# Four of eight pairs of k tiles by seven block products in nine feed-forward groups, with GpSimd making most of the weight sums

## The chip, the cores and the metric

One core of one Trainium2 chip runs the whole kernel. The metric is the device time of one execution in microseconds (us). The engines are TensorE (PE in the profile, its weight loads PEld), VectorE (DVE), ScalarE (ACT), GpSimd (POOL) and SyncE (SP), which issues the weight transfers.

## The reference, cut to what matters

A decoder layer on 256 tokens of width 2048. After the mixer (head groups of mLSTM and retention, one input and one output projection), which the change leaves alone, comes the feed-forward part, of width 5632:

```python
h = rmsnorm(x, g_ffn_pre[l])
ff = (jax.nn.silu(h @ w_gate[l]) * (h @ w_up[l])) @ w_down[l]
x = x + rmsnorm(ff, g_ffn_post[l])
```

All tensors are float32. The change touches only how `h @ w_gate` and `h @ w_up` are computed.

## The kernel before

**Numbers in two parts.** Every float32 matrix product is made from three products of rounded parts. ScalarE rounds a weight tile into `w_hi`, VectorE subtracts (`w_lo = raw - w_hi`), and TensorE adds hi by hi, hi by lo and lo by hi in PSUM. A piece of 1024 weight columns per partition is called a sub; `w_hi` and `w_lo` hold four subs each (`AHEAD` = 4), so ScalarE may round sub m when TensorE has finished sub m-4 (`sub_done`), VectorE follows (`hi_done`), and TensorE follows VectorE (`lo_done`). Each engine works strictly in the order in which the program is written.

**Groups and units.** The feed-forward part has eleven groups of 512 columns of `w_gate` and `w_up`. Group 0 is plain. In groups 1 to 10 the sixteen k tiles (128 rows of the weights each) are taken as eight pairs, the units. A unit's weights are one chunk of `raw` (four chunks, 1 MB each, refilled by SyncE when `lo_done` says that a chunk was used): a quarter each of two `w_up` tiles (blocks b12, b22) and two `w_gate` tiles (b11, b21).

- An R unit is plain: 2 subs, each of 12 matmuls of 512 columns, 24 in all.
- An S unit uses the Strassen-Winograd scheme on the 2x2 blocks (two token tiles by two k tiles, two k tiles by gate and up): 7 block products of 3 matmuls, 21 in all, in 4 subs of 6, 3, 6 and 6 matmuls. The first two subs (b22 and b11, then b21) use the weights as they are. The last two need four sums of weight blocks, which `weight_sums` makes on VectorE, in place in `raw`, after the second sub. Sums of the token tiles are made once (`seven_sums`, `seven_lo`).

Before, `UNITS = "RRSRRSRR"`: two S units in a group, 20 subs. The products of sums gather in their own four PSUM banks over the S units of a group, and `partial_sums` (four VectorE adds of 128x512) folds them after the last S unit; TensorE may start the next group's first matmul only then (`part_done`), since that writes to those banks. The next group's first subs carry the finishing work of the group before: `up_sums`, `gate_sums`, the silu on ScalarE, `gated`, eight TensorE transposes after sub 1 (`turned_ff`), then `turned_hi` and `turned_lo`. The first product of a sum in the next group waits for `turned_lo` (`ff_lo`), which empties the banks of the transposes.

GpSimd does nothing in the feed-forward part but to issue one DMA. After the groups comes the product with `w_down`, plain.

The waits that bind VectorE to ScalarE in an S unit, in `unit_hi`:

```python
act.wait_ge(sub_done, ff_base(i) + (m - 3))
...
act.wait_ge(t_ready, 4 * i + (2 * SEVEN.index(n) + piece - 5))
```

Of the kernel before, what the change touches and what calls it, by code (L numbers as in the profile page):

```python
# [55 lines left out]
UNITS = "RRSRRSRR"  # L56
UNIT_SUBS = {"R": 2, "S": 4}
UNIT_BASE = [sum(UNIT_SUBS[kind] for kind in UNITS[:n]) for n in range(len(UNITS) + 1)]
FF_SUBS = UNIT_BASE[-1]
LAST_S = UNIT_BASE[UNITS.rindex("S") + 1]  # L60
SEVEN = [n for n, kind in enumerate(UNITS) if kind == "S"]
SUB_LIST = [(n, piece) for n, kind in enumerate(UNITS) for piece in range(UNIT_SUBS[kind])]
R_DOWN = R_FF + 2 + (FF_GROUPS - 1) * FF_SUBS // 8
RAW_DOWN = R_FF + 2 * FF_GROUPS
DOWN_SUBS = KF // 2
N_SUBS = 8 * R_DOWN + 4 * DOWN_SUBS
# [26 lines left out]
def ff_base(i):  # L93

    return FF_SUBS * i + (FF_FIRST - FF_SUBS)


def sum_banks(i_odd):

    return (4, 0) if i_odd else (0, 4)  # L100
# [62 lines left out]
def hybrid_layer(nc, x, positions, g_mix_pre, w_in, conv_w, conv_b, b_igate, b_fgate, g_mlstm_head,  # L163
                 g_ret_head, w_out, g_mix_post, g_ffn_pre, w_gate, w_up, w_down, g_ffn_post,
                 inv_freq, out):
    with ExitStack() as ctx:  # L166
# [59 lines left out]
        sb("early_tiles", [P, KF - 8, 2 * SEQ], stack=spare)  # L226
        s_whole = sb("s_whole", [P, 2, 2, SEQ], stack=spare)
        s_sum = sb("s_sum", [P, 2, 4, P], stack=spare)
# [12 lines left out]
        def ff(t):  # L241

            return part[:, 2 * t + 1, :]

# [151 lines left out]
        def _(sp):  # L396
            def load(rnd, q, src, wait=True, free=FREE):

                if wait:
                    sp.wait_ge(lo_done, 8 * (rnd - 1) + free[q])  # L400
# [67 lines left out]
            def second_half(i):  # L468
                for n in range(4, 8):
                    unit_rows(i, n, ff_base(i) + UNIT_BASE[n - 3])  # L470
# [3 lines left out]
            with sp.Fori(1, FF_GROUPS - 1) as i:  # L474
                second_half(i)
                for n in range(4):
                    unit_rows(i + 1, n, ff_base(i) + UNIT_BASE[n + 5])
            second_half(FF_GROUPS - 1)
            for n in range(4 * KF // 4):
                g, k = divmod(n, KF // 4)  # L480
                load(R_DOWN + n // 4, n % 4, rows(w_down, 4 * k, 4, 512 * g, 512))
# [9 lines left out]
        def _(pool):  # L491
# [34 lines left out]
            pool.wait_ge(sub_done, 8 * R_DOWN)  # L526
# [4 lines left out]
        def _(act):  # L531
# [314 lines left out]
            def unit_hi(i, m):  # L846

                n, piece = SUB_LIST[m]
                q, arrived = n % 4, 16 * (n // 4)
                act.wait_ge(sub_done, ff_base(i) + (m - 3))  # L850
                dst, cols = w_hi[:, m % AHEAD, :], slice(SUB * (piece % 2), SUB * (piece % 2 + 1))
                if piece == 0:
                    act.wait_ge(raw_up[q], 32 * i + (arrived - 16))
                if UNITS[n] == "R":
                    if piece == 1:
                        act.wait_ge(raw_full[q], 32 * i + (arrived + 16 * (R_FF + 1)))
                elif piece == 0:
                    act.wait_ge(raw_full[q], 32 * i + (arrived + 16 * (R_FF + 1)))
                    cols = slice(512, 512 + SUB)
                elif piece == 1:  # L860
                    dst, cols = w_hi[:, m % AHEAD, 0:512], slice(512 + SUB, 2 * SUB)
                else:
                    act.wait_ge(t_ready, 4 * i + (2 * SEVEN.index(n) + piece - 5))
                act.activation(dst, raw[:, q, cols], ACT.Copy).then_inc(hi_done, 1)  # L864

            def ff_group(i, odd, first=False):

                _, s0 = sum_banks(odd)
                for m in range(FF_SUBS):
                    unit_hi(i, m)  # L870
                    if m == 0 and first:
                        act.wait_ge(s_summed, 2)
                        for j in range(2):
                            act.activation(s_hi[:, j], s_sum[:, j], ACT.Copy).then_inc(s_rounded, 1)
# [4 lines left out]
                act.activation(part[:, 0, :], bank[:, s0 + 2, :], ACT.Copy).then_inc(p1_out, 1)  # L879
# [5 lines left out]
            ff_group(FF_GROUPS - 1, False)  # L885


            def down_hi(rnd, s):

                rnd, s = rnd + s // 8, s % 8  # L890
                act.wait_ge(raw_full[s // 2], 16 * (rnd + (RAW_DOWN - R_DOWN + 1)))
                act.activation(w_hi[:, s % AHEAD, :], raw_sub(rnd, s)[1], ACT.Copy).then_inc(hi_done, 1)  # L892

            def ahead(rnd, s):

                act.wait_ge(sub_done, 8 * rnd + s + 1)
                down_hi(rnd, s + AHEAD)

            for s in range(-AHEAD, 8):
                ahead(R_DOWN, s)  # L900
# [5 lines left out]
            for g in range(4):  # L906
                full, end = divmod(DOWN_SUBS * (g + 1) - 1, 8)
                with act.Fori(max(3 * g, 1), full) as r:
                    for s in range(8):
                        ahead(r + R_DOWN, s)  # L910
                for s in range(8 if g < 3 else 8 - AHEAD):
                    ahead(R_DOWN + full, s)
# [8 lines left out]
        def _(dve):  # L921
# [429 lines left out]
            def up_sums(i, c0):  # L1351

                dve.wait_ge(part_done, 2 * i)
                dve.wait_ge(sub_done, ff_base(i) + (FF_SUBS - 1))
# [3 lines left out]
            def gate_sums(i, c0):  # L1358

                dve.wait_ge(sub_done, ff_base(i) + FF_SUBS)  # L1360
# [34 lines left out]
            def seven_lo(j):  # L1395
# [20 lines left out]
            def unit_lo(i, m):  # L1416

                n, piece = SUB_LIST[m]
                part_, cols = slice(0, SUB), slice(SUB * (piece % 2), SUB * (piece % 2 + 1))
                if UNITS[n] == "S" and piece < 2:  # L1420
                    cols = slice(512, 512 + SUB) if piece == 0 else slice(512 + SUB, 2 * SUB)
                    part_ = slice(0, SUB) if piece == 0 else slice(0, 512)
                dve.wait_ge(hi_done, ff_base(i) + (m + 1))
                dve.tensor_tensor(w_lo[:, m % AHEAD, part_], raw[:, n % 4, cols],  # L1424
                                  w_hi[:, m % AHEAD, part_].bitcast(F32), ALU.subtract).then_inc(lo_done, 1)
                if UNITS[n] == "S" and piece == 1:
                    weight_sums(i, n)

            def partial_sums(i, s0):
# [3 lines left out]
                dve.wait_ge(sub_done, ff_base(i) + LAST_S)  # L1433
# [8 lines left out]
            def ff_group(i, odd, first=False):  # L1442

                c0, s0 = sum_banks(odd)
                for m in range(FF_SUBS):
                    if m == 2 and not first:
                        up_sums(i - 1, s0)
                    if m == 3 and not first:
                        gate_sums(i - 1, s0)
# [5 lines left out]
                    unit_lo(i, m)  # L1455
                    if m == 1 and first:
                        seven_lo(0)
                    if m == 2 and first:
                        seven_lo(1)
# [8 lines left out]
            for s in range(AHEAD):  # L1468
                lo(R_FF + 1, s + AHEAD)
                if s % 2:  # L1470
                    seven_sums(s // 2)
# [5 lines left out]
            ff_group(FF_GROUPS - 1, False)  # L1477


            for s in range(-AHEAD, 8):  # L1480
                if s == -2:
                    up_sums(FF_GROUPS - 1, 0)
                if s == -1:
                    gate_sums(FF_GROUPS - 1, 0)
                if s == 0:
                    gated(FF_GROUPS - 1)
                lo(R_DOWN, s + AHEAD)
                if s == 1:
# [20 lines left out]
        def _(pe):  # L1509
# [417 lines left out]
```

## Time and profile before

| | us |
|---|---|
| median of 3 runs (lowest, highest) | 1218.34 (1218.07, 1218.73) |
| the profiled execution | 1218.53 |
| its span, first to last instruction | 1216.8 |
| TensorE busy | 1205.2 (99%) |
| VectorE busy | 856.8 (70%) |
| ScalarE busy | 640.5 (53%) |
| GpSimd busy | 15.3 (1%) |

The profiled execution lies 0.2 us from the median, and 1.7 us of it are outside the span. A busy share is an average over all stages; what a stage is worth is read from the stretch of time in which it runs. The feed-forward groups 1 to 10 run from about 530 to 960 us.

### The profile page before, as it was taken

To read this page: it belongs to the slowest core of one execution; us is meant where nothing else is said; L and a number is where in the kernel's file an instruction comes from. 1 tells how busy PE (TensorE), PEld (TensorE's weight loads), DVE (VectorE), ACT (ScalarE), POOL (GpSimd) and SP (SyncE) were. 2 spreads that over 40 slices of the span, in tenths; PEclk is the share of its full clock that TensorE was granted. 3 is DMA by queue.
4 is the path that set the end of the run, shared out by engine and by line. 5 is a ranking of instruction groups with operands and counts; after the bars stand their busy time and mean duration, and the time that the engine had idled before them with its cause. 6 is when DMAs were issued, how large, how long until landed. Compare 5 with 4: busy or idle time off the path is not lost.

```text
span 1216.8 us, 16089 instructions
## 1 busy us (share of the span) xinstructions
PE 1205.2 (99%) x5839; PEld 1012.9 (83%) x5839; DVE 856.8 (70%) x1133; ACT 640.5 (53%) x841; POOL 15.3 (1%) x35
## 2 busy tenths in 40 slices
PE   8999999999999999999999999999999999999997
PEld 7888888888888888888888888888888888888886
DVE  6657877877777655768888888888878844444444
ACT  5654666475664645655455555545555544343432
POOL 2000200000000000000000000000000000000000
PEclk9999999999999999999999999999999999999999
DMA  8657868768686556455556456565645765555651
GB/s 314 211 148 158 206 152 167 171 137 218 160 197 193 198 183 208 161 185 205 175 173 241 142 211 230 176 205 175 211 168 187 262 206 178 205 189 191 203 177 69
DMA packets 121840, 229.59 MB, mean 189 GB/s; under 512 B 7360, under 2 KB 24000, under 8 KB 121280
## 3 DMA queue, kind: packets, MB, share of 16 engines
q1 hardware_dynamic: 121504, 226.85, 60.0%
q0 software_dynamic: 288, 2.10, 0.4%
q8 instruction: 30, 0.49, 0.2%
q14 instruction: 18, 0.15, 0.0%
HBM read 226.83 MB, written 2.10 MB: 188 GB/s over the span
## 4 chain that ended last, share of the span: by engine, by line
PE 98%; DVE 1%; DMA 1%; SPq 0%; ACT 0%; DVEq 0%; issue 0%
PE bank L1511 96%; PE bank L1809 1%; DMA resid<-in_x 1%; PE bank L1516 0%; PE bank L1725 0%; DVE w_lo L934 0%; DVE h L961 0%; DVE resid L1276 0%; PE bank L1782 0%; DVE hT L947 0%; DVE ff_out L1269 0%; ACT bank L749 0%; DVEq L166 0%; ACT hT L586 0%; DVE hT L968 0%
## 5 line engine op out<-in xcount | busy, mean ns | idle before, releaser
L934 DVE TENSOR_TENSOR w_lo<-raw,w_hi 128x1024 fp32r<-128x1024 f32 x260 | 317.2, 1224 | 249.5 <-ACT w_hi L544 128.6
L1511 PE MATMUL bank<-w_hi,h2T 128*128 128x512 f32 x1216 | 383.8, 390 | 0.0
L864 ACT ACTIVATE w_hi<-raw 128x1024 fp32r<-128x1024 f32 x200 | 201.6, 1018 | 197.9 <-PE bank L1511 167.8
L1424 DVE TENSOR_TENSOR w_lo<-raw,w_hi 128x1024 fp32r<-128x1024 f32 x200 | 229.3, 1169 | 65.4 <-ACT w_hi L864 62.7
L544 ACT ACTIVATE w_hi<-raw 128x1024 fp32r<-128x1024 f32 x172 | 181.0, 1059 | 173.9 <-PE bank L1511 156.7
L1511 PE MATMUL bank<-hT,w_hi 128*128 128x512 f32 x768 | 271.7, 397 | 0.0
L1511 PEld LDWEIGHTS bank<-w_hi,h2T 128*128 128x128 f32 x1216 | 228.3, 188 | 47.1
L1511 PE MATMUL bank<-w_lo,h2T 128*128 128x512 f32 x588 | 228.8, 389 | 0.0
L1511 PE MATMUL bank<-w_hi,ffT 128*128 128x512 f32 x704 | 217.3, 389 | 0.0
L1511 PE MATMUL bank<-hT,w_lo 128*128 128x256 f32 x768 | 214.6, 279 | 0.0
L1511 PEld LDWEIGHTS bank<-hT,w_hi 128*128 128x128 f32 x768 | 144.0, 187 | 32.4
L892 ACT ACTIVATE w_hi<-raw 128x1024 fp32r<-128x1024 f32 x88 | 93.4, 1061 | 138.7 <-PE bank L1511 138.6
L1511 PEld LDWEIGHTS bank<-w_hi,ffT 128*128 128x128 f32 x704 | 132.1, 188 | 27.6
L1511 PEld LDWEIGHTS bank<-hT,w_lo 128*128 128x128 f32 x768 | 145.0, 189 | 0.0
L1511 PE MATMUL bank<-w_lo,ffT 128*128 128x512 f32 x352 | 136.9, 389 | 0.0
L1511 PEld LDWEIGHTS bank<-w_lo,h2T 128*128 128x128 f32 x588 | 110.4, 188 | 22.6
L1511 PE MATMUL bank<-w_hi,hT 128*128 128x512 f32 x256 | 81.3, 393 | 0.8 <-DVE w_lo L934 0.8
L1511 PE MATMUL bank<-w_hi,mixT 128*128 128x512 f32 x256 | 80.1, 391 | 0.0
L1511 PEld LDWEIGHTS bank<-w_lo,ffT 128*128 128x128 f32 x352 | 66.1, 188 | 13.5
L1511 PEld LDWEIGHTS bank<-w_hi,hT 128*128 128x128 f32 x256 | 48.1, 188 | 11.4 <-issue 1.2
L1511 PEld LDWEIGHTS bank<-w_hi,mixT 128*128 128x128 f32 x256 | 48.1, 188 | 10.3 <-DVE mixT L1219 0.4
L1511 PE MATMUL bank<-w_lo,hT 128*128 128x512 f32 x128 | 49.8, 389 | 0.0
(203 smaller groups left out, 898.1 us busy)
## 6 DMA issues: line engine op xcount, KB each, us to landing
raw<-in_w_in SPq DMA_DIRECT2D x63, 1024.0 KB, 10.2
raw<-in_w_down SPq DMA_DIRECT2D x44, 1024.0 KB, 5.0
raw<-in_w_up SPq DMA_DIRECT2D x80, 512.0 KB, 4.0
raw<-in_w_gate SPq DMA_DIRECT2D x80, 512.0 KB, 4.9
raw<-in_w_out SPq DMA_DIRECT2D x16, 1024.0 KB, 5.0
raw<-in_w_gate SPq DMA_DIRECT2D x4, 1024.0 KB, 5.3
raw<-in_w_up SPq DMA_DIRECT2D x4, 1024.0 KB, 6.6
resid<-in_x SPq DMA_DIRECT2D x2, 1024.0 KB, 7.2
```

The lines of the kernel that those rows point to most:

```text
L544: act.activation(part_of(w_hi, rnd, s), src, ACT.Copy).then_inc(hi_done, 1)
L864: act.activation(dst, raw[:, q, cols], ACT.Copy).then_inc(hi_done, 1)
L892: act.activation(w_hi[:, s % AHEAD, :], raw_sub(rnd, s)[1], ACT.Copy).then_inc(hi_done, 1)
L934: dve.tensor_tensor(part_of(w_lo, rnd, s), raw_sub(rnd, s)[1], part_of(w_hi, rnd, s).bitcast(F32), ALU.subtract).then_inc(lo_done, 1)
L1424: dve.tensor_tensor(w_lo[:, m % AHEAD, part_], raw[:, n % 4, cols], w_hi[:, m % AHEAD, part_].bitcast(F32), ALU.subtract).then_inc(lo_done, 1)
L1511: return pe.matmul(out_, lhsT, rhs, start=start, stop=stop, skip_group_check=True)
L1809: ins = pe.transpose(bank[:, b0 + j // 2, c:c + P], ff(t)[:, j * P:(j + 1) * P], ident)
```

## The change

- `UNITS` becomes a `Plan` per group: `RSRSRSSR` in groups 1 to 9 (four S units, the last two in a row, 24 subs) and `RSRSRRRR` in group 10 (two S units, 20 subs).
- The sums are made in another order: b12 = b22 - b12 first, as soon as the chunk has landed and without a wait for the subs; b11 = b12 + b11 after the unit's first sub; b21 = b21 - b11 after the second; b22 = b22 - b11. Third and fourth sub take the blocks in another pairing.
- GpSimd makes all four sums in the S units 1, 3 and 5, and b12 and b22 in unit 6. VectorE makes b11 and b21 of unit 6. That is 14 sums of a group on GpSimd and 2 on VectorE, where 8 were on VectorE. The sums of group 10 are all GpSimd's.
- ScalarE's rounding of an S unit's third sub waits for b11 and b21, the fourth for b22 (in unit 6: b12 and b11, then b22 and b21).
- `partial_sums` of group i is no longer at the end of its group on VectorE but in group i+1, between the subs 0 and 1; ScalarE's copy of the first product moves likewise.
- The wait for `turned_lo` stands before the fourth sub of the first S unit, which is sub 5 of the group (before: before its first sub, sub 4).
- Token sums are made for four pairs instead of two, once.
- The loads wait for the chunk's use by the new counts.

The core of the diff:

```diff
-UNITS = "RRSRRSRR"
+SEVEN = (1, 3, 5, 6)
+SUMS_BY_POOL = (4, 4, 4, 2)
...
+FULL = Plan("RSRSRSSR")
+FINAL = Plan("RSRSRRRR")
...
+            def weight_sums(i, j):
+
+                n = SEVEN[j]
+                b12, b22, b11, b21 = (raw[:, n % 4, 512 * c:512 * (c + 1)] for c in range(4))
+                made = sums_made(i, j)
+                pool.wait_ge(raw_up[n % 4], 32 * i + 16 * (n // 4 - 1))
+                pool.tensor_tensor(b12, b22, b12, ALU.subtract).then_inc(t_ready, 1)
+                if j == 3:
+                    pool.wait_ge(t_vector, 2 * i - 1)
+                    pool.tensor_tensor(b22, b22, b11, ALU.subtract).then_inc(t_ready, 1)
+                    return
+                pool.wait_ge(lo_done, ff_base(i) + (FULL.base[n] + 1))
+                pool.wait_ge(t_ready, made + 1)
+                pool.tensor_tensor(b11, b12, b11, ALU.add).then_inc(t_ready, 1)
+                pool.wait_ge(lo_done, ff_base(i) + (FULL.base[n] + 2))
+                pool.wait_ge(t_ready, made + 2)
+                pool.tensor_tensor(b21, b21, b11, ALU.subtract).then_inc(t_ready, 1)
+                pool.tensor_tensor(b22, b22, b11, ALU.subtract).then_inc(t_ready, 1)
...
+                elif piece >= 2 and j == 3:
+                    act.wait_ge(t_ready, sums_made(i, j) + (piece - 1))
+                    act.wait_ge(t_vector, 2 * i + (piece - 3))
+                elif piece >= 2:
+                    act.wait_ge(t_ready, sums_made(i, j) + (piece + 1))
...
-                dve.wait_ge(lo_done, ff_base(i) + (UNIT_BASE[n] + 2))
-                dve.tensor_tensor(b11, b12, b11, ALU.subtract).then_inc(t_first, 1)
-                dve.wait_ge(t_first, 4 * i + (2 * j - 3))
-                dve.tensor_tensor(b12, b22, b12, ALU.subtract).then_inc(t_first, 1)
-                dve.wait_ge(t_first, 4 * i + (2 * j - 2))
-                dve.tensor_tensor(b22, b22, b11, ALU.subtract).then_inc(t_ready, 1)
-                dve.wait_ge(t_ready, 4 * i + (2 * j - 3))
-                dve.tensor_tensor(b21, b21, b22, ALU.subtract).then_inc(t_ready, 1)
...
-                for m in range(FF_SUBS):
+                for m in range(plan.subs):
+                    if m == 1 and not first:
+                        partial_sums(i - 1, FULL, c0)
                     if m == 2 and not first:
-                        up_sums(i - 1, s0)
+                        up_sums(i - 1, FULL, s0)
...
-                partial_sums(i, s0)
...
+                    pe.wait_ge(lo_done, ff_base(i) + (m + 1))
+                    if first and piece == 3:
+                        pe.wait_ge(ff_lo, 2 * i)
```

Where the weight sums stand. VectorE before, second S piece of the first S unit of a group in the loop and the sums behind it (`raw<-raw`):

```order
L1424 TENSOR_TENSOR w_lo<-raw,w_hi 128x512
L1408 TENSOR_TENSOR raw<-raw 128x512
L1409 ISA
L1410 TENSOR_TENSOR raw<-raw 128x512
L1411 REGISTER_ALU
L1412 TENSOR_TENSOR raw<-raw 128x512
L1414 TENSOR_TENSOR raw<-raw 128x512
```

GpSimd after, the first S unit of a group in its loop (before, there was nothing):

```order
L583 TENSOR_TENSOR raw<-raw 128x512
L588 ISA
L589 ISA
L590 TENSOR_TENSOR raw<-raw 128x512
L591 REGISTER_ALU
L592 REGISTER_ALU
L593 TENSOR_TENSOR raw<-raw 128x512
L594 TENSOR_TENSOR raw<-raw 128x512
```

The four sums have moved to GpSimd; on VectorE the third sub's subtraction now stands directly behind the second's.

The start of a group on VectorE, before (the first row that writes `part` is `up_sums`):

```order
L1424 TENSOR_TENSOR w_lo<-raw,w_hi 128x1024
L1423 REGISTER_ALU
L1424 TENSOR_TENSOR w_lo<-raw,w_hi 128x1024
L1353 ISA
L1354 ISA
L1356 TENSOR_TENSOR part<-part,bank 128x512 x2
L1423 REGISTER_ALU
L1424 TENSOR_TENSOR w_lo<-raw,w_hi 128x1024
```

and after:

```order
L1494 TENSOR_TENSOR w_lo<-raw,w_hi 128x1024
L1515 ISA
L1517 TENSOR_TENSOR part<-part,bank 128x512
L1518 ISA
L1519 TENSOR_TENSOR part<-part,bank 128x512
L1521 TENSOR_TENSOR part<-part,bank 128x512
L1522 TENSOR_TENSOR part<-part,bank 128x512
L1492 REGISTER_ALU
L1494 TENSOR_TENSOR w_lo<-raw,w_hi 128x1024
L1439 REGISTER_ALU
L1441 TENSOR_TENSOR part<-part,bank 128x512 x2
```

The four adds of `partial_sums` (L1517 to L1522) now stand between the first two subs of the next group, ahead of `up_sums` (L1441).

## Rows read from the trace of the kernel before

**Rows 1.** The page: busy time by engine, and the chain that ended last.

```profile
PE 1205.2 (99%) x5839; PEld 1012.9 (83%) x5839; DVE 856.8 (70%) x1133; ACT 640.5 (53%) x841; POOL 15.3 (1%) x35
...
PE 98%; DVE 1%; DMA 1%; SPq 0%; ACT 0%; DVEq 0%; issue 0%
```

**Rows 2.** Busy time of each engine in one whole group of the loop.

```profile
core 0: us, PE busy (x) PEld busy (x) DVE busy (x) ACT busy (x) POOL busy (x), PEclk, DMA share, GB/s
651.30:694.36 43.06, 43.06 (x196) 35.74 (x195) 35.83 (x41) 22.96 (x25) 0.00 (x0) 1.00 0.57 195
```

**Rows 3.** The same view for 60 us of the `w_down` stage, plain matmuls only.

```profile
1000.00:1060.00 60.00, 60.00 (x266) 49.67 (x266) 28.17 (x24) 24.68 (x27) 0.00 (x0) 1.00 0.58 193
```

**Rows 4.** VectorE's instructions by form in that group: line, shapes, count | busy, mean ns.

```profile
L1424 DVE TENSOR_TENSOR w_lo<-raw,w_hi 128x1024 fp32r<-128x1024 f32 x18 | 21.6, 1222 | 4.1 <-ACT w_hi L864 3.9
...
L1424 DVE TENSOR_TENSOR w_lo<-raw,w_hi 128x512 fp32r<-128x512 f32 x2 | 1.4, 693 | 2.1 <-ACT w_hi L864 2.1
L1410 DVE TENSOR_TENSOR raw<-raw 128x512 f32<-128x512 f32 x2 | 1.4, 693 | 0.1
```

**Rows 5.** VectorE in order of time around a group's start: start, duration, instruction, idle before.

```profile
659.08 0.68 DVE L1435 TENSOR_TENSOR part<-part,bank 128x512 f32<-128x512 f32 x1
...
661.12 0.68 DVE L1440 TENSOR_TENSOR part<-part,bank 128x512 f32<-128x512 f32 x1
661.72 1.22 DVE L1424 TENSOR_TENSOR w_lo<-raw,w_hi 128x1024 fp32r<-128x1024 f32 x1
...
667.72 1.28 DVE L1362 TENSOR_TENSOR part<-part,bank 128x512 f32<-128x512 f32 x2 [0.30 <-PE bank L1511]
668.92 1.22 DVE L1424 TENSOR_TENSOR w_lo<-raw,w_hi 128x1024 fp32r<-128x1024 f32 x1
670.05 1.41 DVE L1370 SCALAR_TENSOR_TENSOR part<-part,stat 128x512 f32<-128x512 f32 x2
...
677.34 1.28 DVE L1378 TENSOR_TENSOR ffT<-bank,ffT 128x512 f32 x2
```

**Rows 6.** ScalarE in order of time in the same group.

```profile
679.57 1.06 ACT L864 ACTIVATE w_hi<-raw 128x1024 fp32r<-128x1024 f32 x1 [1.65 <-PE bank L1511]
...
693.26 1.06 ACT L864 ACTIVATE w_hi<-raw 128x1024 fp32r<-128x1024 f32 x1 [2.94 <-DVE raw L1412]
```

**Rows 7.** GpSimd by form: its instructions on float32 in SBUF (busy us, mean ns).

```profile
L504 POOL MEMSET wg_both<- 128x2048 f32 x1 | 1.8, 1794 | 0.0
L501 POOL TENSOR_SCALAR_AFFINE_SELECT sel<-sel 8x1024 f32<-8x1024 f32 x1 | 1.1, 1086 | 0.0
...
L499 POOL TENSOR_SCALAR_AFFINE_SELECT columns<-columns 128x128 f32<-128x128 f32 x1 | 0.3, 292 | 0.1
```

**Rows 8.** GpSimd in order of time, 143 to 152 us.

```profile
143.04 1.78 POOL L519 TENSOR_SCALAR_AFFINE_SELECT decay<-decay 128x128 f32<-128x128 f32 x6 [134.71 <-ACT decay L657]
...
149.16 1.59 POOL L519 TENSOR_SCALAR_AFFINE_SELECT decay<-decay 128x128 f32<-128x128 f32 x1 [0.67 <-ACT decay L657]
...
151.13 0.47 POOL L519 TENSOR_SCALAR_AFFINE_SELECT decay<-decay 128x128 f32<-128x128 f32 x1
```

**Rows 9.** VectorE in order of time, 148 to 152 us.

```profile
148.59 0.87 DVE L1151 SCALAR_TENSOR_TENSOR gT<-pre,columns,gT 128x256 f32<-128x256 f32 x2
149.38 1.21 DVE L934 TENSOR_TENSOR w_lo<-raw,w_hi 128x1024 fp32r<-128x1024 f32 x1
150.51 0.94 DVE L1151 SCALAR_TENSOR_TENSOR gT<-pre,columns,gT 128x256 f32<-128x256 f32 x2
```

**Rows 10.** GpSimd and VectorE near 6 us.

```profile
5.90 2.25 POOL L506 TENSOR_SCALAR_AFFINE_SELECT rel<-rel 128x128 f32<-128x128 f32 x1
...
5.72 2.27 DVE L961 COPY h<-resid 128x512 f32<-128x512 f32 x4 [4.41 <-DMA resid<-in_x]
```

More of the change, by code:

```diff
@@ L55, with __init__ @@
 FF_FIRST = 8 * (R_FF + 2)
-UNITS = "RRSRRSRR"
[L57 to L64, printed above, removed]
+SEVEN = (1, 3, 5, 6)
+SUMS_BY_POOL = (4, 4, 4, 2)
+class Plan:
+    def __init__(self, units):
+        self.units = units
+        self.size = [4 if kind == "S" else 2 for kind in units]
+        self.base = [sum(self.size[:n]) for n in range(len(units) + 1)]
+        self.subs = self.base[-1]
+        self.after_seven = self.base[units.rindex("S") + 1]
+        self.pieces = [(n, piece) for n in range(len(units)) for piece in range(self.size[n])]
+FULL = Plan("RSRSRSSR")
+FINAL = Plan("RSRSRRRR")
+DOWN_FIRST = FF_FIRST + (FF_GROUPS - 2) * FULL.subs + FINAL.subs
+R_DOWN = R_FF + 2 * FF_GROUPS
 DOWN_SUBS = KF // 2
-N_SUBS = 8 * R_DOWN + 4 * DOWN_SUBS
+N_SUBS = DOWN_FIRST + 4 * DOWN_SUBS
 SPLIT_OUT = AHEAD
@@ L93, in ff_base, with sum_banks, ff_slot, sums_made @@
 def ff_base(i):
-    return FF_SUBS * i + (FF_FIRST - FF_SUBS)
-def sum_banks(i_odd):
-    return (4, 0) if i_odd else (0, 4)
+    return FULL.subs * i + (FF_FIRST - FULL.subs)
+def sum_banks(odd):
+    return (4, 0) if odd else (0, 4)
+def ff_slot(odd, m):
+    return (m + (0 if odd else FULL.subs)) % AHEAD
+def sums_made(i, j):
+    per_group = sum(SUMS_BY_POOL)
+    return per_group * i + (sum(SUMS_BY_POOL[:j]) - per_group)
+def down_slot(n):
+    return (DOWN_FIRST + n) % AHEAD
 def event_of(rnd, unit):
@@ L396, in _, with load @@
         def _(sp):
-            def load(rnd, q, src, wait=True, free=FREE):
+            def load(rnd, q, src, wait=True, free=FREE, counted=None):
                 if wait:
-                    sp.wait_ge(lo_done, 8 * (rnd - 1) + free[q])
+                    sp.wait_ge(lo_done, (8 * rnd if counted is None else counted) - 8 + free[q])
                 k = src.shape[1]
@@ L909, in _ @@
                     for s in range(8):
-                        ahead(r + R_DOWN, s)
+                        ahead(r, s)
                 for s in range(8 if g < 3 else 8 - AHEAD):
-                    ahead(R_DOWN + full, s)
+                    ahead(full, s)
                     if s == end:
@@ L1429, in partial_sums, with unit_lo @@
-            def partial_sums(i, s0):
+            def unit_lo(i, odd, plan, m):
+                n, piece = plan.pieces[m]
+                q, slot = n % 4, ff_slot(odd, m)
+                dve.wait_ge(hi_done, ff_base(i) + (m + 1))
+                if plan.units[n] == "R":
+                    dve.tensor_tensor(w_lo[:, slot, :], raw[:, q, SUB * piece:SUB * (piece + 1)],
+                                      w_hi[:, slot, :].bitcast(F32), ALU.subtract).then_inc(lo_done, 1)
+                    return
+                j = SEVEN.index(n)
+                dve.tensor_tensor(slot_blocks(w_lo, slot, piece), seven_blocks(piece, j, q),
+                                  slot_blocks(w_hi, slot, piece).bitcast(F32), ALU.subtract)\
+                   .then_inc(lo_done, 1)
+                if j == 3 and piece < 2:
+                    _, _, b11, b21 = (raw[:, q, 512 * c:512 * (c + 1)] for c in range(4))
+                    dve.wait_ge(lo_done, ff_base(i) + (m + 1))
+                    if piece == 0:
+                        dve.wait_ge(t_ready, sums_made(i, j) + 1)
+                        dve.tensor_tensor(b11, raw[:, q, 0:512], b11, ALU.add).then_inc(t_vector, 1)
+                    else:
+                        dve.wait_ge(t_vector, 2 * i - 1)
+                        dve.tensor_tensor(b21, b21, b11, ALU.subtract).then_inc(t_vector, 1)
@@ L1440, in partial_sums, with ff_group @@
                 dve.tensor_tensor(x, u3, p5, ALU.add).then_inc(part_done, 1)
-            def ff_group(i, odd, first=False):
+            def ff_group(i, odd, plan=FULL, first=False):
                 c0, s0 = sum_banks(odd)
-                for m in range(FF_SUBS):
+                for m in range(plan.subs):
+                    if m == 1 and not first:
+                        partial_sums(i - 1, FULL, c0)
                     if m == 2 and not first:
-                        up_sums(i - 1, s0)
+                        up_sums(i - 1, FULL, s0)
                     if m == 3 and not first:
-                        gate_sums(i - 1, s0)
+                        gate_sums(i - 1, FULL, s0)
                     if m == 4:
```

200 lines of the change are left out of this document (108 added, 92 removed).

## The prediction

> **What bounds the kernel now.** I read the page first: busy time and the chain that ended last [rows 1]. TensorE is busy for 99% of the span and makes up 98% of the chain, so before the change no wait costs anything and time falls only if TensorE gets fewer matmuls. Then I took one whole group [rows 2]: 43.06 us, TensorE busy in all of it at the full clock of 2.4 GHz (granted clock 1.00), VectorE for 35.8 us (83%), ScalarE for 23.0, GpSimd not at all. VectorE is the engine with the least room: 7.2 us a group. Its forms [rows 4] and its order at a group's start [rows 5] show what that room consists of: waits for ScalarE, which itself waits for TensorE to free a slot [rows 6], since `w_hi` holds four subs. So the reader should see a TensorE that never waits, and behind it a chain ScalarE, VectorE, TensorE that is at most four subs ahead.
>
> **TensorE.** The plain stage has 266 matmuls in 60 us [rows 3], 0.2256 us each. A group before has 6 R units of 24 and 2 S units of 21, 186 matmuls, 42.0 us; with the eight transposes that makes the 43.06. After, 4 x 24 + 4 x 21 = 180, so 6 fewer: 1.35 us less, 41.7 us. Over nine groups 54 matmuls, **12.2 us less** on the path that sets the end. Group 10 and all else keep their matmuls. This is all that the change can give: 1218.5 (the profiled execution, 0.2 from the median) - 12.2 = 1206.3.
>
> **VectorE's work.** In one group: eight sums of 0.69 us go (-5.6), two more S units add two subtractions of 1024 columns at 1.2 (21.6 / 18) and two of 512 at 0.69 (+3.8) [rows 4], two sums stay with VectorE (+1.4). So 35.8 - 5.6 + 3.8 + 1.4 = 35.4 us in a group of 41.7. By work alone VectorE would still fit. The token sums of two more pairs, made once, lie in a stretch in which VectorE is half idle: nothing.
>
> **A sum on GpSimd.** The trace has no GpSimd instruction with two inputs. The nearest: a select with one input takes 0.292 us for 128 columns and 1.086 for 1024 [rows 7], so 0.886 ns a column, and 512 columns would take 0.63 us. That is the lower bound. If the second input costs as much again, it is 0.63 + 512 x 0.886 = 1.09 us, the upper bound. I take 1.09: a memset of 2048 columns, which reads nothing, takes 0.876 ns a column [rows 7], so GpSimd seems to handle one thing a column at about that pace and a second operand should add to it. The Trainium skill, GPSIMD Engine Reference, Performance versus the Vector engine, gives 4497 ns for 2048 float32 of a two-input operation and says that the two reads share one port; a quarter of it would be 1.12 us, an estimate by that page, and no run here shows it yet. By it each group would be some 0.2 us longer than below.
>
> **Do GpSimd and VectorE hinder each other?** Six selects take 1.78 us while VectorE is idle, 0.3 each. One that starts at 149.16 takes 1.59 us and ends at 150.75 [rows 8]; within it VectorE subtracts two SBUF operands from 149.38 to 150.59, at its usual 1.21 [rows 9]. Near 6 us a select of the same size takes 2.25 us and ends with four VectorE copies [rows 10]. Behind 150.5 the two alternate: selects of 0.47, and two VectorE instructions with two SBUF inputs in 0.94 instead of 0.87 [rows 8, 9]. So one waits while the other reads. A select reads only 128 columns, so VectorE lost little; a sum would read 1024 values a partition. The bounds of what a sum costs VectorE when they meet are thus 0 and its whole 1.09. The Trainium skill, SBUF — State Buffer, Who interferes with whom, says that a VectorE instruction with two SBUF inputs and a GpSimd instruction that reads SBUF share one read interface, and that whoever has it keeps it for the whole instruction. The trace agrees as far as it goes (0.29 to 1.59 us for the select); by that rule it is the upper bound. This speaks against the change: 24 of VectorE's subtractions, its two sums and `gated` are of that kind.
>
> **The order on VectorE in an S unit.** Before, the sums filled the time between the second sub's subtraction and the third's with VectorE's own work. Now that time is a wait: GpSimd makes b11 (behind VectorE's second subtraction, which blocks it), then b21, then ScalarE rounds (1.06, [rows 6]) and VectorE goes on. In units 3 and 5 nothing else stands between in VectorE's order: 2 x 1.09 + 1.06 + 0.1 for hand-offs (an allowance) = 3.3 us each, 6.7. In unit 1 `gate_sums` covers b11, and `gated` (1.41, [rows 5]) lies in the wait; b21 waits behind its first half (0.7), then 1.09 + 1.06 + 0.1 less the second half 0.7 gives 1.5, and b22, which begins with that second half's end, keeps VectorE for another 0.7: 2.2. Queued behind these waits are all later subtractions, and TensorE waits for them. Sum: 35.4 + 6.7 + 2.2 = 44.3 us. In unit 6 GpSimd's b22 meets the subtractions of the second and third sub: 1.1, so 45.4. The four early sums b12 can start at any time: 0 if they find VectorE waiting (or if VectorE's queued instructions go first, as the four copies did), 4 x 1.09 if each meets a subtraction (alternation, as behind 150.5). I take half, since both are in the rows: 2.2. **VectorE's group is 47.6 us**, between 45.4 and 49.8. That is above TensorE's 41.7, so VectorE's order sets the pace, and the four subs of lead don't help since the lead is used up in every group.
>
> **The start of a group.** `partial_sums` (2.7 us, 659.08 to 661.8, [rows 5]) ended 5.9 us ahead of the group's start at 667.7; moved behind sub 0 it needs the last S unit and ends about when TensorE wants the banks. With `gate_sums` ready only at the group's start, the chain `gate_sums`, silu, `gated`, third sub, fourth sub, `turned_lo` has to end before sub 5, 10 us in; before, `turned_lo` ended at 678.6, 10.9 in, against a need 11.9 in. Where VectorE sets the pace this is in the sum above. Where it doesn't, it is late by about 0.9 us (third rival).
>
> **ScalarE and transfers.** ScalarE gets two more roundings of 1.06 and two of 0.63, 3.4 us on 23.0: hidden by its room of 18 us. The bytes stay 8.4 MB a group; the loads' waits follow the same subs, and the DMA share is 0.57. Nothing.
>
> **Forecast.** 47.6 - 43.06 = 4.5 us more in each of nine groups: 1218.5 + 9 x 4.5 = **1259 us**; its bounds 45.4 and 49.8 give 1240 and 1279.
>
> **Rivals.**
> - *All hidden, TensorE sets the pace: 1206.* Needs sums near 0.63 us that don't block, and a start of the group that is never late. For it: VectorE's work of 35.4 under 41.7. Against: the blocked selects, and the chains above, which in the best case (0.63, no blocking) still hold TensorE for 0.7 us a group at sub 5: then 42.4, -0.66 x 9, 1212.
> - *Long sums, no blocking: 1216.* The wait in units 3 and 5 is 1.09 x 2 - 0.69 + 1.06 + 0.1 = 2.65, in unit 1 0.85: 35.4 + 5.3 + 0.85 = 41.6, level with TensorE's 41.7. Then two places make TensorE wait. Of the two S units in a row, the second's first rounding can start only when TensorE is through the first's first sub; rounding, subtraction, sum, subtraction, sum, subtraction are 1.06 + 1.2 + 0.69 + 0.69 + 0.69 + 1.2 = 5.5, against 24 matmuls or 5.4: 0.1 to 0.3. And `turned_lo` is 0.9 late. 42.8 a group, -0.25 x 9: 1216, no change that could be told.
> - *Short sums that do block: 1222 to 1236.* Waits of 2 x 0.63 + 1.16 = 2.4 twice, 1.3 in unit 1, collisions of 0.6 to 3.2: 35.4 + 4.8 + 1.3 = 41.5, with collisions 42.1 to 44.7, and the late start of up to 0.9 on top where TensorE is level: 43.5 to 45.
> - *The last case taken further: every sum meets a subtraction and each costs 1.2 instead of 1.09*: 49.8 + 14 x 0.1 = 51.2, +8.1 x 9, 1291.
>
> The other side of my forecast is the first rival; the point where it turns is a VectorE group of 43.06 us, which is at sums of about 0.6 us with collisions, or 1.1 without.
>
> **How the numbers follow.** Blocking and long sums, 1240 to 1279, 0.52, further up to 1291 0.06. Short sums that block, 0.10. Long sums that don't, 1216, 0.12, half of it within the band. The cases of 1206 to 1214, 0.20. About 0.2% (2.4 us) is what a measurement can tell from no change. Faster 0.25, same 0.07, slower 0.68. The range reaches from 1210, which takes in most of the faster cases, to 1284; outside lie about 0.1 below and 0.06 above.
>
> **What would show it.** Right: groups of 46 to 50 us with TensorE waiting for `w_lo`, GpSimd's sums of 512 columns at 1.1 us or more (longer where a subtraction lies beside them), subtractions beside sums longer than 1.22, VectorE waiting some 3 us before the third sub of units 3 and 5, and the chain no longer 96% matmuls. Wrong: subtractions that stay at 1.22 us beside GpSimd's sums, sums under 0.8 us, or groups of 41.7 to 42.9 with TensorE busy throughout.

## The result

| | us |
|---|---|
| before, median of 4 runs (lowest, highest) | 1218.53 (1218.07, 1218.86) |
| after, median of 4 runs (lowest, highest) | 1283.05 (1282.05, 1284.23) |
| ratio, 95% interval | 1.052 (1.050 to 1.054) |

The changed kernel is 64.5 us slower. Forecast were 1259 and a range of 1210 to 1284: the sign and the mechanism hold, the loss was put at 40.5 us and is 1.6 times that. The median lies 1 us inside the upper end of the range, and above the 1240 to 1279 of the main case.

### The profile page after: what moved, and what is told of

It is laid out like the page before. It is cut to its first block, busy times and chain, and to the rows that moved or that the text cites. A ratio compares the mean times of both kernels' runs of the same rounds, so it can differ in the third digit from the quotient of the medians.

```text
span 1282.5 us, 16409 instructions
## 1 busy us (share of the span) xinstructions
PE 1218.0 (95%) x5785; PEld 1006.1 (78%) x5785; DVE 907.8 (71%) x1121; ACT 662.5 (52%) x879; POOL 231.5 (18%) x169
## 4 chain that ended last, share of the span: by engine, by line
PE 59%; DVE 16%; issue 12%; POOL 6%; ACT 3%; DMA 3%; DVEq 0%; POOLq 0%; SPq 0%; ACTq 0%
PE bank L1600 58%; DVE w_lo L1498 6%; DVE w_lo L1494 3%; POOL raw L594 3%; DMA raw<-in_w_in 2%; POOL raw L593 2%; ACT w_hi L944 2%; DVE w_lo L1019 1%; DVE part L1447 1%; DMA resid<-in_x 1%; POOL raw L590 1%; DVE part L1441 1%; DVE ffT L1463 1%; DVE raw L1509 1%; DVE part L1519 0%
## 5 line engine op out<-in xcount | busy, mean ns | idle before, releaser
L1600 PE MATMUL bank<-w_hi,h2T 128*128 128x512 f32 x1036 | 333.0, 391 | 0.0
L1019 DVE TENSOR_TENSOR w_lo<-raw,w_hi 128x1024 fp32r<-128x1024 f32 x172 | 209.3, 1223 | 127.3 <-ACT w_hi L620 126.7
L620 ACT ACTIVATE w_hi<-raw 128x1024 fp32r<-128x1024 f32 x172 | 180.6, 1059 | 174.8 <-PE bank L1600 154.2
L1498 DVE TENSOR_TENSOR w_lo<-raw,w_hi 128x1024 fp32r<-128x1024 f32 (+1 forms) x152 | 204.6, 1364 | 75.9 <-ACT w_hi L944 74.7
L944 ACT ACTIVATE w_hi<-raw 128x1024 fp32r<-128x1024 f32 (+1 forms) x152 | 142.9, 951 | 197.4 <-POOL raw L593 95.9
L1600 PEld LDWEIGHTS bank<-w_hi,h2T 128*128 128x128 f32 x1036 | 195.2, 188 | 41.7
L1600 PE MATMUL bank<-w_lo,h2T 128*128 128x512 f32 x498 | 194.2, 390 | 0.0
L1564 DVE TENSOR_TENSOR w_lo<-raw,w_hi 128x1024 fp32r<-128x1024 f32 x88 | 107.9, 1226 | 121.3 <-ACT w_hi L980 121.3
L980 ACT ACTIVATE w_hi<-raw 128x1024 fp32r<-128x1024 f32 x88 | 93.4, 1061 | 138.7 <-PE bank L1600 138.7
L1600 PEld LDWEIGHTS bank<-w_lo,h2T 128*128 128x128 f32 x498 | 93.9, 189 | 19.9
L1494 DVE TENSOR_TENSOR w_lo<-raw,w_hi 128x1024 fp32r<-128x1024 f32 x84 | 99.4, 1215 | 10.1 <-ACT w_hi L932 10.0
L583 POOL TENSOR_TENSOR raw<-raw 128x512 f32<-128x512 f32 x38 | 78.9, 2075 | 127.7 <-DMA raw<-in_w_up 127.7
L932 ACT ACTIVATE w_hi<-raw 128x1024 fp32r<-128x1024 f32 x84 | 85.0, 1050 | 21.5 <-PE bank L1600 21.5
L1600 PE MATMUL bank<-w_hi,s_more 128*128 128x512 f32 x144 | 59.6, 455 | 28.9 <-DVE w_lo L1498 28.9
L590 POOL TENSOR_TENSOR raw<-raw 128x512 f32<-128x512 f32 x29 | 43.3, 1493 | 227.3 <-DVE w_lo L1498 227.3
```

The lines of the kernel that those rows point to most:

```text
L583: pool.tensor_tensor(b12, b22, b12, ALU.subtract).then_inc(t_ready, 1)
L590: pool.tensor_tensor(b11, b12, b11, ALU.add).then_inc(t_ready, 1)
L620: act.activation(part_of(w_hi, rnd, s), src, ACT.Copy).then_inc(hi_done, 1)
L932: act.activation(w_hi[:, ff_slot(odd, m), :], raw[:, q, SUB * piece:SUB * (piece + 1)], ACT.Copy).then_inc(hi_done, 1)
L944: act.activation(slot_blocks(w_hi, ff_slot(odd, m), piece), seven_blocks(piece, j, q), ACT.Copy).then_inc(hi_done, 1)
L980: act.activation(w_hi[:, down_slot(s), :], raw_sub("down", s)[1], ACT.Copy).then_inc(hi_done, 1)
```

## The profile after

The page of the changed kernel, busy time and the chain that ended last:

```profile
PE 1218.0 (95%) x5785; PEld 1006.1 (78%) x5785; DVE 907.8 (71%) x1121; ACT 662.5 (52%) x879; POOL 231.5 (18%) x169
...
PE 59%; DVE 16%; issue 12%; POOL 6%; ACT 3%; DMA 3%; DVEq 0%; POOLq 0%; SPq 0%; ACTq 0%
```

Against [rows 1] there are 54 matmuls fewer, as planned, but they are 59% of the chain and no longer 98%. One group, from one `partial_sums` to the next, answers to [rows 2]:

```profile
core 0: us, PE busy (x) PEld busy (x) DVE busy (x) ACT busy (x) POOL busy (x), PEclk, DMA share, GB/s
735.13:785.44 50.31, 44.71 (x189) 35.30 (x188) 41.25 (x39) 25.36 (x30) 22.66 (x14) 0.97 0.50 167
```

The group takes 50.3 us instead of 43.06, and TensorE waits in it. VectorE is busy for 41.25 us and idle for 9.1. What fills both shows in its order of time, units 3, 5 and 6 and then the next group's start, which answers to [rows 5]:

```profile
714.39 1.81 DVE L1498 TENSOR_TENSOR w_lo<-raw,w_hi 128x1024 fp32r<-128x1024 f32 x2
719.84 4.61 DVE L1498 TENSOR_TENSOR w_lo<-raw,w_hi 128x1024 fp32r<-128x1024 f32 x3 [3.63 <-ACT w_hi L944]
724.58 0.69 DVE L1506 TENSOR_TENSOR raw<-raw 128x512 f32<-128x512 f32 x1
725.19 0.68 DVE L1498 TENSOR_TENSOR w_lo<-raw,w_hi 128x512 fp32r<-128x512 f32 x1
726.02 1.57 DVE L1509 TENSOR_TENSOR raw<-raw 128x512 f32<-128x512 f32 x1
727.51 3.42 DVE L1498 TENSOR_TENSOR w_lo<-raw,w_hi 128x1024 fp32r<-128x1024 f32 x2
730.85 2.35 DVE L1494 TENSOR_TENSOR w_lo<-raw,w_hi 128x1024 fp32r<-128x1024 f32 x2
...
741.23 1.28 DVE L1447 TENSOR_TENSOR part<-part,bank 128x512 f32<-128x512 f32 x2
742.43 0.90 DVE L1498 TENSOR_TENSOR w_lo<-raw,w_hi 128x512 fp32r<-128x512 f32 x1
743.25 2.44 DVE L1455 SCALAR_TENSOR_TENSOR part<-part,stat 128x512 f32<-128x512 f32 x2
746.26 3.89 DVE L1498 TENSOR_TENSOR w_lo<-raw,w_hi 128x1024 fp32r<-128x1024 f32 x2 [0.57 <-ACT w_hi L944]
```

and GpSimd beside it:

```profile
715.77 1.58 POOL L590 TENSOR_TENSOR raw<-raw 128x512 f32<-128x512 f32 x1 [4.65 <-DVE w_lo L1498]
717.43 1.28 POOL L593 TENSOR_TENSOR raw<-raw 128x512 f32<-128x512 f32 x1
718.67 1.30 POOL L594 TENSOR_TENSOR raw<-raw 128x512 f32<-128x512 f32 x1
719.93 2.30 POOL L583 TENSOR_TENSOR raw<-raw 128x512 f32<-128x512 f32 x1
725.35 1.68 POOL L586 TENSOR_TENSOR raw<-raw 128x512 f32<-128x512 f32 x1 [3.13 <-DVE raw L1506]
727.35 1.35 POOL L583 TENSOR_TENSOR raw<-raw 128x512 f32<-128x512 f32 x1 [0.32 <-DMA raw<-in_w_up]
...
741.48 1.29 POOL L590 TENSOR_TENSOR raw<-raw 128x512 f32<-128x512 f32 x1 [12.78 <-DVE w_lo L1498]
```

Below, a *meeting* is a sum on GpSimd that falls together with a VectorE instruction that has two SBUF inputs.

- Two subtractions of 1024 columns take 2.35 us with GpSimd idle (L1494 at 730.85). With a b12 (L583) beside them they take 3.42, and b12 takes 2.30 where it has to let VectorE go first. Three take 4.61 with a b12 beside them, two with b22 and b12 beside them 3.89, `gated` 2.44 instead of 1.41, a sum of VectorE's 1.57 instead of 0.69.
- Between the second sub's subtraction and the third's in unit 5 VectorE idles 3.63 us (b11, b21, rounding), likewise 3.64 in unit 3.
- `gate_sums` (L1447, one input from PSUM) takes its usual 1.28 beside b11, and b11 its shortest, 1.29. So an instruction with one input from SBUF and one from PSUM isn't held up; the ones that are have two from SBUF, as in [rows 8, 9].
- An undisturbed sum takes 1.29 us, not 1.09.

Where TensorE waits in the changed kernel from 701.01 to 751.3 us, a stretch of one group's length (total us, times, longest):

```profile
PE bank L1600 <- DVE w_lo L1498: 3.8, 3, 2.8
PE bank L1600 <- DVE ffT L1463: 1.7, 1, 1.7
```

The longest is in the pair of S units in a row, the 1.7 is the wait for `turned_lo` at the first S unit. Behind the longest, the granted clock of TensorE is 0.50, its lower level of 1.2 GHz, for some 3 us, and its matmuls start 0.43 us apart instead of 0.23. ScalarE then waits for the slot, and VectorE for ScalarE. The lines are TensorE's matmul in order of time, the row of that stretch, VectorE's subtraction in order of time, and the row of another group:

```profile
729.84 0.79 PE L1600 MATMUL bank<-w_hi,s_more 128*128 128x512 f32 x1 [2.77 <-DVE w_lo L1498]
729.80:732.90 3.10, 3.06 (x7) 2.48 (x8) 3.10 (x3) 0.86 (x2) 0.00 (x0) 0.50 0.22 28
733.98 1.23 DVE L1494 TENSOR_TENSOR w_lo<-raw,w_hi 128x1024 fp32r<-128x1024 f32 x1 [0.79 <-ACT w_hi L932]
635.45:684.89 49.44, 44.35 (x193) 34.83 (x192) 41.05 (x39) 26.16 (x30) 23.70 (x14) 1.00 0.48 163
```

In that other group the clock stayed at 1.00. Of the eight intervals between the `partial_sums` of groups 1 to 9, three are like it, 49.4 us each; the five with 0.97 take 50.2 to 50.35. So the clock is a third cost beside the waits and the meetings, 0.9 us in the groups in which it falls, and the prediction has no term for it.

## The experiments

The theory: VectorE's order sets the pace of a group, stretched by two things, the waits for GpSimd's chain and the time for which GpSimd's reads keep VectorE out. Rivals: one of the two does nothing; the plan itself (four S units, `partial_sums` in the next group) is what costs; VectorE is overloaded and GpSimd's help only too small. The first four kernels cross the two causes and then take GpSimd away. Each of e1 to e6 is a single execution. Those of e1 to e4 stood beside one of the kernel before at 1218.15 us, e5 to e8 beside 18 of it, median 1219.23 (1218.33 to 1223.95). Group times are counted from one `partial_sums` to the next; a mean is over the eight intervals of groups 1 to 9.

**e1_neither.** GpSimd's sums and all waits for them are left out.

```diff
-            with pool.Fori(1, FF_GROUPS - 1) as i:
-                for j in range(4):
-                    weight_sums(i, j)
-            for j in range(2):
-                weight_sums(FF_GROUPS - 1, j)
...
                 elif piece >= 2 and j == 3:
-                    act.wait_ge(t_ready, sums_made(i, j) + (piece - 1))
                     act.wait_ge(t_vector, 2 * i + (piece - 3))
-                elif piece >= 2:
-                    act.wait_ge(t_ready, sums_made(i, j) + (piece + 1))
```

> Leaves out all sums of weight blocks that GpSimd makes, and every wait for them; VectorE's two sums of unit 6 stay, the plan of four S units too. My theory (VectorE's order is stretched by waits for GpSimd and by GpSimd holding the read side): nothing is left that stretches it, VectorE has 35.4 us of work in a group, TensorE sets the pace at 41.7 to 42.1 us a group, 1206 to 1210 us in all. Rival (the plan itself costs, by partial_sums in the next group's start and by two S units in a row): groups of 43 us or more, 1218 or more.

Measured: 1211.73 us, 1.7 above what was expected, before beside it 1218.15. The group:

```profile
703.67:745.92 42.25, 41.98 (x190) 34.52 (x189) 34.71 (x39) 25.83 (x30) 0.00 (x0) 1.00 0.58 199
```

So the plan alone does not cost; it is worth 6.4 us, half of the 12.2 that the matmuls promise. The group is 42.25 and not 41.7, because TensorE waits once in it, before the third sub of unit 6, the second of the two in a row:

```profile
740.73 0.39 PE L1571 MATMUL bank<-w_hi,h2T 128*128 128x512 f32 x1
741.38 0.50 PE L1571 MATMUL bank<-w_hi,s_more 128*128 128x512 f32 x1 [0.27 <-DVE w_lo L1470]
741.72 0.40 PE L1571 MATMUL bank<-w_lo,s_more 128*128 128x512 f32 x1
```

The starts are 0.65 and 0.34 us apart instead of 0.23 each: 0.54 us a group for a wait that is listed with 0.27. The list counts from the end of the matmul before, 741.12, but the next would have started at 740.96; and the first matmul behind the wait takes 0.50 us instead of 0.39, so that the second comes late too. Nine times that is 4.9 of the missing 5.8 us.

**e2_port_only.** GpSimd makes its 14 sums of two constant tiles into one that nothing reads while the groups run; no other engine waits for them, and the real sums are left out. (GpSimd also waits for its own last sum each time.)

```diff
-                pool.tensor_tensor(b12, b22, b12, ALU.subtract).then_inc(t_ready, 1)
+                pool.tensor_tensor(resid[:, 1, 0:512], h2T[:, 0, :].bitcast(F32), h2T[:, 1, :].bitcast(F32), ALU.add).then_inc(t_ready, 1)
```

> GpSimd makes 14 sums of 512 columns in a group at the times of the changed kernel, but of two constant tiles into a tile that nobody reads, and neither ScalarE nor VectorE waits for them; so the real sums are left out and only the traffic stays. Theory of blocking: each sum that meets a subtraction costs VectorE 1.1 us as in the changed kernel; with 10 to 13 meetings VectorE's group is 35.4 + 11 to 14 = 46 to 50 us, 1245 to 1280 in all. Rival (the waits for GpSimd are the cost, the blocking is not): subtractions stay at 1.22 us, 1206 to 1215.

Measured: 1281.92 us, almost the 1283.05 of the whole change and 2 above what was expected. A group in which the granted clock is 0.97 as in the one above (with 1.00 it takes 48.97):

```profile
734.81:784.70 49.89, 44.06 (x187) 34.85 (x186) 44.72 (x40) 25.34 (x30) 24.39 (x14) 0.97 0.52 176
```

VectorE's busy time goes from 34.7 to 44.7 us with not one instruction more. Its subtractions in S units, by form over 200 us:

```profile
L1503 DVE TENSOR_TENSOR w_lo<-raw,w_hi 128x1024 fp32r<-128x1024 f32 x49 | 87.8, 1811 | 16.6 <-ACT w_hi L949 16.6
```

They take 1.81 us in the mean instead of 1.22. The blocking alone makes a loss of this size; the rival that it costs nothing is out.

**e3_wait_only.** Each sum becomes one of 2 columns and a memset of 1256, which writes and reads nothing; all waits stay, the real sums are left out.

```diff
-                pool.tensor_tensor(b12, b22, b12, ALU.subtract).then_inc(t_ready, 1)
+                pool.tensor_tensor(resid[:, 0, 0:2], h2T[:, 0, 0:2].bitcast(F32), h2T[:, 1, 0:2].bitcast(F32), ALU.add)
+                pool.memset(resid[:, 1, 0:1256], 0.0).then_inc(t_ready, 1)
```

> Every GpSimd sum is replaced by a sum of 2 columns and a memset of 1256 (about 1.2 us together, almost without reads), with all waits of the changed kernel; the real sums are left out and only the waiting stays. Theory: subtractions stay at 1.22 us, VectorE waits 3.4 us before the third sub of units 3 and 5 and 1 to 2 us in unit 1, group 43.5 to 45 us, 1222 to 1236 in all. Rival (the waits alone make the loss): 50 us, 1275 or more. Rival (blocking alone): 42, 1210 or less.

Measured: 1236.38 us, 0.4 above the upper end of what was expected. The group, and the subtractions:

```profile
715.58:760.15 44.57, 42.83 (x190) 34.34 (x189) 34.61 (x40) 25.32 (x29) 21.89 (x28) 1.00 0.57 188
```
```profile
L1511 DVE TENSOR_TENSOR w_lo<-raw,w_hi 128x1024 fp32r<-128x1024 f32 x54 | 65.6, 1223 | 42.5 <-ACT w_hi L957 40.7
```

GpSimd is busy for 21.9 us a group here too, but writing does not touch VectorE: 1.22 us. GpSimd itself is still held up at each short read, up to 1.03 us for a sum of 2 columns that takes 0.19 alone, much as b11 is in the changed kernel (1.58 instead of 1.29); that belongs to the waits here. The waits alone cost 2.3 us a group against e1. The costs do not add: the mean groups are 42.29 in e1, 49.43 in e2, 44.57 here and 49.98 in the changed kernel, so 7.1 for blocking, 2.3 for waits and 7.7 for both. With the waits, VectorE is idle while GpSimd makes b11 and b21, so these meet nothing; without them they meet subtractions. VectorE's busy and idle times say so: 44.7 and 5.2 us in e2, 41.25 and 9.1 in the changed kernel.

**e4_vector4.** The same plan with all 16 sums of a group on VectorE.

```diff
+                if piece == 0:
+                    dve.tensor_tensor(b12, b22, b12, ALU.subtract).then_inc(t_ready, 1)
+                    dve.wait_ge(lo_done, ff_base(i) + (m + 1))
+                    dve.wait_ge(t_ready, made + 1)
+                    dve.tensor_tensor(b11, b12, b11, ALU.add).then_inc(t_ready, 1)
+                if piece == 1:
+                    dve.wait_ge(lo_done, ff_base(i) + (m + 1))
+                    dve.wait_ge(t_ready, made + 2)
+                    dve.tensor_tensor(b21, b21, b11, ALU.subtract).then_inc(t_ready, 1)
+                    dve.tensor_tensor(b22, b22, b11, ALU.subtract).then_inc(t_ready, 1)
```

> The plan of four S units with all 16 sums of a group on VectorE, GpSimd idle; b12 and b11 behind the first sub's subtraction, b21 and b22 behind the second's. Theory: 14 more sums of 0.72 us on VectorE are 10.1 us, but no meeting and short waits (0.4 us in each of four units): 35.4 + 10.1 + 1.6 = 47 us a group, 1245 to 1258 in all, so that even VectorE alone is faster than with GpSimd's help. Rival (GpSimd's sums unload VectorE, the loss is of the plan): 1285 or more.

Measured: 1257.18 us, 26 less than with GpSimd's help. The group:

```profile
720.55:768.13 47.58, 44.05 (x190) 35.63 (x189) 43.67 (x53) 25.92 (x30) 0.00 (x0) 0.96 0.53 176
```

The 47 expected comes out, but as 43.7 us of work and 3.9 of waiting where 45.5 and 1.6 were expected, and the clock has a part in it: two of the eight groups keep it at 1.00 and take 46.0 us, the other six take 47.5 to 47.6. VectorE is busy for longer than in the changed kernel (43.67 against 41.25) but idle for less (3.9 against 9.1). Against e1 a group costs in the mean 4.9 us more when VectorE makes the 14 sums, and 7.7 when GpSimd does. In e2, where nobody waits, even VectorE's busy time is longer than here, 44.72. With four S units VectorE's work alone is above TensorE's 41.7 us when it makes all sums itself.

**e5_b12_vector.** Only b12 moves to VectorE.

```diff
-                pool.tensor_tensor(b12, b22, b12, ALU.subtract).then_inc(t_ready, 1)
...
+                if piece == 0:
+                    dve.wait_ge(lo_done, ff_base(i) + (m + 1))
+                    dve.tensor_tensor(b12, b22, b12, ALU.subtract).then_inc(t_vector, 1)
```

> The changed kernel with one kind of sum moved: VectorE makes b12 of all four S units of groups 1 to 9 (and of the two of group 10), behind the first sub's subtraction; GpSimd keeps b11, b21 and b22 of units 1, 3 and 5 and b22 of unit 6, and all waits for them stay. Theory of blocking: four meetings of 1.1 us a group go and four sums of 0.7 us come, so VectorE has MORE work and yet the group is 1 to 2 us shorter: 1264 to 1274. Rival (VectorE is simply overloaded and GpSimd's b12 unloads it): 4 x 0.7 us more a group, 1290 to 1308.

Measured: 1272.60 us, 10 less than the changed kernel, with 2.8 us more work of VectorE's own in each group; the mean group is 1.4 us shorter. A group's rows:

```profile
680.75:729.63 48.88, 44.30 (x186) 34.53 (x185) 39.91 (x44) 24.63 (x30) 14.69 (x10) 0.97 0.52 177
```

VectorE is busy for 39.9 us instead of 41.25: 2.8 more for four sums and, by difference, 4.1 less for the four meetings that are gone. Idle stays at 9.0.

**e6_port_half.** As e2, with 256 columns in each sum instead of 512.

> As e2_port_only, but GpSimd's 14 sums of a group have 256 columns instead of 512; real sums and waits left out as there. If a meeting costs VectorE the time for which GpSimd reads, it costs half, 0.5 to 0.6 us, some 5 us a group instead of 10, of which part now fits into VectorE's room: 1215 to 1245. Rival (a meeting costs a fixed time, whatever is read): above 1265.

Measured: 1230.53 us. The group and one of GpSimd's lines (shortest, median and longest ns):

```profile
712.25:756.37 44.12, 42.84 (x189) 34.38 (x189) 37.41 (x40) 25.94 (x29) 15.43 (x14) 1.00 0.57 190
```
```profile
L598 POOL TENSOR_TENSOR resid<-h2T x29: 736/747/1182, 544.0 to 951.9; 128x256 f32<-128x256 f32 x29
```

Half the reading leaves 18.8 of the 70.2 us that e2 lost against e1, and VectorE's busy time grows by 2.7 us, not 10. The same place in e6 and in e2, two subtractions with one sum of GpSimd's beside them:

```profile
706.03 2.89 DVE L1503 TENSOR_TENSOR w_lo<-raw,w_hi 128x1024 fp32r<-128x1024 f32 x2
728.06 3.43 DVE L1503 TENSOR_TENSOR w_lo<-raw,w_hi 128x1024 fp32r<-128x1024 f32 x2
```

Against the 2.35 of an undisturbed pair the meeting costs 0.54 with 256 columns and 1.08 with 512, so its price goes by what is read. That the total is less than half is the number of meetings: at these prices, an estimate, 2.7 us are five of them and 10 are nine. In units 3 and 5 of e6 most sums fall into times in which VectorE waits for ScalarE.

**e7_three_end and e8_three_late.** Three S units and all their sums on VectorE (as in e4), GpSimd idle.

```diff
-SEVEN = (1, 3, 5, 6)
-FULL = Plan("RSRSRSSR")
-FINAL = Plan("RSRSRRRR")
+SEVEN = (2, 4, 6)
+FULL = Plan("RRSRSRSR")
+FINAL = Plan("RRSRSRRR")
```

That is e8; e7 has SEVEN = (1, 3, 5), RSRSRSRR and RSRSRRRR, and `partial_sums` at the end of its own group.

> Three S units in groups 1 to 9 (RSRSRSRR), all 12 sums of a group on VectorE, GpSimd idle, partial_sums at the end of the group as before the change. TensorE has 183 matmuls a group, 42.4 us with the transposes, VectorE 19 x 1.2 + 3 x 0.69 + 12 x 0.72 + 7.6 = 41.1 us of work. Theory: level, so small waits of TensorE remain: 43.06 - 0.68 + 0 to 0.8 a group, 1212 to 1220. Rival (an S unit right behind the group's start makes TensorE wait for gated and turned_lo, as in e4_vector4): 1222 to 1235.

> Three S units as RRSRSRSR, all sums on VectorE, partial_sums between sub 0 and 1 of the next group: the finishing work of a group then meets two R units, not an S unit. Same work as e7_three_end. Theory that the group's start is what is left: 1211 to 1216, faster than both kernels. Rival (VectorE's 41.1 us of work are too many wherever they stand): 1218 or more.

Measured: e7 1212.97 us (9 executions, 1212.64 to 1217.31), ratio to before 0.9949 (0.9934 to 0.9964); e8 1212.87 us (10, 1212.34 to 1216.75), 0.9946 (0.9931 to 0.9960). **Both beat both kernels**, by 0.5% against before. The group of e8:

```profile
704.20:746.60 42.40, 42.40 (x192) 35.17 (x192) 39.32 (x47) 24.55 (x28) 0.00 (x0) 1.00 0.58 198
```

TensorE is busy throughout, at 42.40 us where 183 matmuls and the transposes make 42.4, and VectorE's work is 39.3 us, not 41.1. Where the S units and `partial_sums` stand makes no difference here, so the rival of the group's start falls, and with it the theory of e8 that the start is what is left.

## Why the prediction was right in sign and short in size

- **TensorE 41.7 us a group.** The count was right. In e1 it was 42.25: the pair of S units in a row makes TensorE wait, which the prediction had put at 0.1 to 0.3 us in its rival without blocking; it is listed with 0.27 and costs 0.54. Even with sums for nothing the change gives 6.4 us, so the 1206 of the first rival was out of reach. Its best case, 1212, is e1's number by luck: it rested on a wait at sub 5 that e1 doesn't have.
- **VectorE's work of 35.4 us.** It was 34.7 in e1: right within 2%.
- **GpSimd and VectorE shut each other out.** Right, shown by e2 against e3: reading costs VectorE time, writing doesn't. The price of a meeting, taken as up to a sum's length, 1.09, is 1.07 to 1.1 us (3.42 - 2.35).
- **A sum on GpSimd, 1.09 us.** This term was too small. The select's rate was taken once for each operand. The runs have 0.19 us for 2 columns (the shortest in e3), 0.736 for 256 and 1.29 for 512: 0.18 us + 2.16 ns a column, 2.4 times the select's 0.886 and not twice. The upper bound was no bound. The prediction's other estimate, 1.12, is low as well; a quarter of a long sum leaves out most of the fixed 0.18.
- **Waits of 3.3 us in units 3 and 5.** They are 3.64 and 3.63; the difference is nearly the 2 x 0.2 by which the sums are longer.
- **Unit 1, 2.2 us.** Idle 0.57, the second sub's subtraction + 0.21, `gated` + 1.03, the next two subtractions + 1.54 together, of which some 1.1 are a b12: 2.25. Right.
- **The early sums b12: half of 4 x 1.09.** This is the largest mis-sizing. All four meet a subtraction in every group: one starts when the last b22 ends, and just then VectorE comes back from its wait (719.84 and 719.93). They cost 4.4 us instead of 2.2. The four copies of [rows 10], which went first one after another, were read as a chance that VectorE's queue goes first; with subtractions the two alternate, as behind 150.5 in [rows 8, 9].
- **b22 of unit 6, 1.1 us.** It was 0.9 (1.57 - 0.69), at VectorE's own sum b21 and not at a subtraction.
- **The sum again:** 34.7 + 7.3 + 2.25 + 4.4 + 0.9 = 49.5, measured 49.4 in the groups with the clock at 1.00. The others have 0.9 more, by the clock. The mean, 49.98, is 6.9 over the 43.07 before.
- **The whole.** Against e1, which has the same plan, the eight intervals lose 61.5 us, the first group 8.4 (its `partial_sums` starts at 585.11 instead of 576.75) and the last interval 3.0 (44.08 instead of 41.12). That adds up to 72.9, against 72.5 between the profiled executions. The plan by itself had given 6.4.
- **Luck in the range.** The measured time lies where the prediction put the case that every sum meets a subtraction, 1279 to 1291, with a chance of 0.06. That isn't what happened: eight of the fourteen sums meet VectorE at a price, the six b11, b21 and b22 of units 3 and 5 fall into its waits. The range ended at 1284 and one of the four executions, 1284.23, is outside.
- **A sum that doesn't follow.** The rival of short sums that block gives 42.1 to 44.7 and up to 0.9 more, which isn't the 43.5 to 45 that it goes on with. Nothing in the forecast hangs on it.
- **Where the budget misleads.** It added waits and meetings as if independent. e2 and e3 show 7.1 and 2.3 for them apart and 7.7 together. The sum came out since the meetings were counted in the order with the waits. Taking the waits away, which the budget says gives 8.9 us a group, gave 0.55.
- **The start of the group.** `turned_lo` does hold TensorE (1.7 us), but not for the reason in the forecast. In e1, with `partial_sums` at the same place, that wait is gone, so the 0.9 by which it was said to be late without any blocking isn't there. It comes with the blocking (1.7 in e2) and also with the waits alone (1.0 in e3).

## What to carry over

Before giving work to an idle engine, ask what it shares with the busy one: here 14 sums that VectorE could make in 0.69 us each took 0.7 us each of its time (10 us in e2) although GpSimd made them, and e4 was faster without the help. Cross the two costs of a helper, its waits and its traffic, in two kernels before arguing about either, for they need not add. And where an engine's room is 7 us a group, spend that and no more: three S units take 3.5 of it and win, and with four VectorE's order is longer than TensorE's work whoever makes the sums.

## What the runs showed of the hardware

- A GpSimd sum with two SBUF inputs takes 0.18 us + 2.16 ns a column of 128 partitions (0.19, 0.736 and 1.29 us for 2, 256 and 512 columns), where one of VectorE's of 512 takes 0.69.
- While it reads, a VectorE instruction with two SBUF inputs is held up by 1.07 us (512 columns) or 0.54 (256); one with an input from PSUM is not (1.28 beside 1.29), and GpSimd's memsets hold up nothing (1.223 beside 21.9 us of them a group). The Trainium skill, SBUF — State Buffer, Who interferes with whom, states this division; the runs agree in all three cases.
- In the groups, when both have work queued, they take turns by instruction (719.84 and 719.93), so the loss of each is close to the other's length. The four copies of [rows 10], which have one input, went ahead of a select together.
- A wait of TensorE that is listed with 0.27 us moved the next matmuls by 0.54 (e1).
- After a wait of TensorE of 2.77 us its granted clock was 0.50 for 3.1 us, and the group was 0.9 us longer than those in which it stayed at 1.00.
